# Row-tiled matmuls in the looped MLP chunks of a three-block fp32 transformer kernel

## The chip, the cores and the metric

The kernel runs on one core of one Trainium2 chip. The metric is the device time of one launch in microseconds (us); lower is better. Three runs of the kernel before gave a median of 978.46 us (978.15 to 979.44).

## The reference

Sequence 256, width 1024, everything in fp32. A first block has two layers (attention, then an MLP), a second block has one layer (sparse attention and retention, then a gated FFN). The change touches the MLPs of the two layers of the first block, and nothing else that is computed:

```python
D_MODEL = 1024; SEQ = 256; D_FF = 4 * D_MODEL

def _sq_relu_mlp(h, w_up, w_down):
    u = jax.nn.relu(h @ w_up)          # 256 x 1024 @ 1024 x 4096
    return (u * u) @ w_down            # 256 x 4096 @ 4096 x 1024

x = x + _sq_relu_mlp(_rmsnorm(x, a_norm_mlp[i]), a_w_up[i], a_w_down[i])   # layer 0
x = x + _sq_relu_mlp(_rmsnorm(x, b_norm_mlp[j]), b_w_up[j], b_w_down[j])   # layer 1
```

## The kernel before

Precision. Each fp32 operand is split into a high and a low part, both of type fp32r, which the TensorE multiplies in one pass. A product is three matmuls: high by high, high by low, low by high. Of the weights, ScalarE makes the high part (`split_hi`, L1182; in the loops `split_hi_loop`, L1190, with its instruction at L1194; tile `whi`) and VectorE the low part (`split_lo`, L1689, instruction at L1693; tile `wlo`).

Units. Weights come in units of 512 rows by 512 columns, 1 MB each, over a ring of four slots (`RING = 4`) of three buffers, `raw`, `whi` and `wlo`. SyncE issues the loads. A unit is split three units ahead of its use (`AHEAD = 3`). `prev[u]` is the unit that held the slot before u; the high part of u may be written when the semaphore `mul_done` says that prev[u] has been multiplied (two increments for each unit), and a new load into `raw` waits for both parts of prev[u].

The MLP. D_FF is walked in 8 chunks of 512 (`CHUNKS`). `mlp_units` (L639) orders the units: up(j+1), two units (contraction halves h = 0 and 1), then down(j), two units (output halves c = 0 and 1). up(0) and down(7) are made outside of the loop, by `up_first` and by `mlp_end` (L677). The 7 chunks between are made by `mlp_chunk`, one function for each engine: chunk 0 written out, 1 to 5 in a hardware loop, 6 written out. With two layers that is 14 chunks. "Chunk" below always means one of these 14.

A chunk on TensorE (`mlp_chunk`, L1453). The up part makes the hidden values transposed: for each h, `up_pair` (L1438) fills the two banks of the pair `proj` (Pp), then the two banks of the pair `turn` (Tp). The stationary operand is a 128x128 piece of the weights. For each bank and each k of four, L1445 streams 512 columns (the activations' high and low part side by side) against the high weights; then L1449 streams 256 columns (high activations alone) against the low weights. So a chunk has 32 matmuls of 512 columns and 32 of 256 in its up part. The down part (`half_unit`, L1409, through `products`, L1403, the lines L1405 to L1407) has, for each of two output halves (banks `score` for c = 0, `outp` for c = 1), two token tiles and four k, three matmuls of 512 columns: 48 in all. The stationary operand is there a piece of the activations, and the sums stay in the banks over the chunks. Each of these matmuls contracts 128 rows, uses the whole array, and has a weight load of its own ahead of it.

Around it. When a pair of up banks is complete, ScalarE copies its cross terms (`copy_crosses`, L1216) and VectorE adds, applies relu and squares (`square_relu`, L1708 and L1711); ScalarE and VectorE write the squares' high and low part as the operand of down (`squares_hi`, L1222; `squares_lo`, L1719). TensorE waits for `up_added` before it fills a pair again, for `up_lo` before down(j), and for `lo_done` before each unit.

Of the kernel before, what the change touches and what calls it, by code (L numbers as in the profile page):

```python
# [31 lines left out]
P = 128  # L32
# [6 lines left out]
UK = 4  # L39
# [24 lines left out]

GAINS = ["a_mem_norm", "b_mem_norm", "a_norm_attn", "a_norm_mlp", "kv_norm", "b_norm_attn",
# [34 lines left out]
def build(nc, A, out):  # L100

    UNITS = []

    def unit(w, rows, cols, nk=UK):
# [27 lines left out]
    count.up = 0  # L132
    free = {}

    def add(kind):
        st = Step()
        st.kind = kind
        STEPS.append(st)
        return st

    ctx = ExitStack()
    with ctx:
# [101 lines left out]
        up_copied = sem("up_copied")  # L244
        up_added = sem("up_added")
# [47 lines left out]
        def turn_operand(src, half, gains, ready, set_free, cols=None):  # L293

            st = add("turn_operand")
            st.src, st.half, st.gains, st.ready, st.set_free = src, half, gains, ready, set_free
            st.use, st.hi = [t_use(), t_use()], count.hi
            count.hi += 2
            return st.use
# [31 lines left out]
        def evacuate(u, pieces, scale, slot_free=None, silu=False, bank="P"):  # L331

            st = add("evacuate")
            st.u, st.pieces, st.scale, st.chunk = u, pieces, scale, count.chunk
            st.slot_free, st.silu, st.bank = slot_free, silu, bank
            for t in range(NT):
                free[bank, t] = (chunk_evac, 2 * count.chunk + t + 1)
            count.chunk += 1
            return st

        def rope_chunk(u, slot, table, scale, slot_free, bank="P"):

            st = add("rope_chunk")
            st.u, st.slot, st.table, st.scale, st.slot_free, st.bank = u, slot, table, scale, slot_free, bank
            st.rope, st.read = count.rope, count.rope_read
            for t in range(NT):
                free[bank, t] = (rope_read, 2 * count.rope_read + t + 1)
            count.rope += 1
            count.rope_read += 1
            return st  # L350

        def rope(slot, n, table):
            st = add("rope")
            st.slot, st.n, st.table, st.chunk, st.rope = slot, n, table, count.chunk, count.rope
            count.rope += 1
            return st

        def turn_heads(src, blocks, pieces, ready):

            st = add("turn_heads")  # L360
            st.src, st.blocks, st.pieces, st.ready = src, blocks, pieces, ready
            st.use = [t_use(), t_use()]
            return st.use

        LOW, HIGH, ALL = slice(0, DH), slice(DH, P), slice(0, P)
        tok = lambda t: slice(t * P, (t + 1) * P)
# [65 lines left out]

        def norm(pair):

            st = add("diff_norm")
            st.items, (st.oss, st.ors) = pair, pair[0].both

        def residual(half, bank, u, scale):
            st = add("residual")
            st.half, st.bank, st.u, st.scale, st.r = half, bank, u, scale, count.resid  # L440
            count.resid += 2
            for t in range(NT):
                free[bank, t] = (resid_done, st.r + t + 1)
            return st

        def statistics(src, ready, factor=None, kind="plain"):


            st = add("statistics")
            st.src, st.ready, st.n, st.ss, st.rs = src, ready, count.rstd, col(2), col(2)  # L450
            st.what, st.factor = kind, factor
            if kind == "final":
                st.ss2, st.r2 = col(2), col(2)
            st.sums = count.ss
            count.ss += 2 if kind == "final" else 1
# [195 lines left out]
        def mlp(w_up, w_down, hset, use0, r1, gain):  # L651
# [16 lines left out]
            st.base, st.hset, st.uset, st.up0 = base, hset, 1 - hset, count.up  # L668
# [111 lines left out]
        small = add("small_norm")  # L780
        small.chunk, small.ss, small.rs = ev.chunk, col(2), col(2)
# [45 lines left out]
        def select(ix, first, last):  # L827

            st = add("select")
            st.st, st.rounds = ix, (first, last)  # L830
# [9 lines left out]
        kava = add("shared_kv")  # L840
        kava.use, kava.s, kava.ss, kava.rs = sn_use, s_use((kava_done, 1)), col(2), col(2)
# [36 lines left out]
        qn = add("query_norm")  # L878
        qn.chunk, qn.ss, qn.rs = ev.chunk, col(16), col(16)
        split(qa[1] + AHEAD)  # L880
        last = retention_out(3)
        group = add("group_center")
        group.o, group.mu, group.va, group.rs = last[1], col(16), col(16), col(16)
# [207 lines left out]
        def _(pool):  # L1091
# [19 lines left out]
            sums = [0]  # L1111

            def inverse_of_sums(dst, ss, n, eps=EPS):

                sums[0] += 1
                pool.wait_ge(sum_done, sums[0])
                inverse_rms(dst, ss, n, eps).then_inc(inverse_done, 1)

            for st in STEPS:
# [42 lines left out]
                elif st.kind == "query_norm":  # L1162
                    inverse_of_sums(st.rs, st.ss, DH)
                elif st.kind == "small_norm":
                    inverse_of_sums(st.rs, st.ss, P)
                elif st.kind == "shared_key_sum":
                    inverse_of_sums(st.st.rs, st.st.ss, DH)
                elif st.kind == "group_sum":
                    inverse_of_sums(st.st.rs, st.st.va, DH, GN_EPS)
# [11 lines left out]
        def _(act):  # L1181
            def split_hi(u):  # L1182
# [3 lines left out]
                if prev[u] is not None:  # L1186
                    act.wait_ge(mul_done, 2 * prev[u] + 2)
                act.activation(shaped(whi, u), shaped(raw, u), ACT.Copy).then_inc(hi_done, 1)  # L1188

            def split_hi_loop(u, j, j0, per):  # L1190

                act.wait_ge(landed[slot[u]], j * 32 + (32 * fills[u] - 32 * j0))
                act.wait_ge(mul_done, j * (2 * per) + (2 * prev[u] + 2 - 2 * per * j0))
# [62 lines left out]
            for st in STEPS:  # L1256
# [6 lines left out]
                elif st.kind == "statistics":  # L1263
# [3 lines left out]
                    for t in range(NT):  # L1267
                        ins = act.activation(junk[:, t, :], st.src[:, t, :], ACT.Square, accum_out=st.ss[:, t:t + 1])  # L1268
                    ins.then_inc(ss_done, 1)
# [6 lines left out]
                elif st.kind == "turn_operand":  # L1276
                    for b in range(2):
                        n = st.use[b]
                        act.wait_ge(t_full, n + 1)
                        if st.set_free and b == 0:  # L1280
                            act.wait_ge(mul_done, st.set_free)
                        for g, s, k0 in st.gains:
                            k = k0 + 2 * b
                            if g is None:
                                ins = act.activation(set_hi[s][:, k:k + 2, :], Tb[n % 2][:], ACT.Copy)
                            else:
                                kk = 4 * st.half + 2 * b
                                act.wait_ge(gain_cols, 1 if g < FIRST * KT else 3)
                                for i in range(2):
                                    ins = act.activation(set_hi[s][:, k + i, :], Tb[n % 2][:, i * TOK:(i + 1) * TOK],  # L1290
                                                         ACT.Copy, scale=gcol[:, g + kk + i:g + kk + i + 1])
                        ins.then_inc(t_hi, 1)
                elif st.kind == "evacuate":
                    act.wait_ge(rstd_done, st.scale.n_done)
                    for t in range(NT):
                        act.wait_ge(mul_done, 2 * st.u + t + 1)
                        if st.slot_free and t == 0:
                            act.wait_ge(t_full, st.slot_free)
                        for i, ((a, b), dst) in enumerate(st.pieces):
# [772 lines left out]
```

## Time and profile before

| | |
|---|---|
| median of 3 runs | 978.46 us |
| profiled execution | 978.28 us |
| its span, first to last instruction | 976.6 us |
| mean granted TensorE clock | 0.99 |
| TensorE busy with matmuls | 938.0 us, 96% |
| TensorE busy with weight loads | 790.2 us, 81% |
| VectorE / ScalarE / GpSimd busy | 587.7 / 476.0 / 70.8 us |
| read from memory | 156.12 MB, 161 GB/s |

The profiled execution took 978.28 us, of which 976.6 us are its span. A matmul's record is longer than its share of the engine, because matmuls are pipelined: the record of 512 columns lasts 0.39 us, while the next one starts much earlier. What one matmul costs is therefore read from the distance between starts, or from the chain of waits, where a piece lasts until the next one begins. Weight loads have rows of their own (PEld), beside the matmuls (PE).

### The profile page before, as it was taken

Reading aid. Unit: us, or ns where it says so; the run is one execution under the profiler, and the core shown is the slowest. Engines: PE = TensorE matmul, PEld = TensorE weight load, DVE = VectorE, ACT = ScalarE, POOL = GpSimd, SP = SyncE. Lnnn points to the kernel's source line nnn. Section 1 sums busy time; section 2 is a strip of 40 time slices with the busy share of each in tenths; the row PEclk is TensorE's granted clock in tenths of the full one; section 3 lists DMA queues with packets and bytes.
Section 4 is the critical chain, followed back from the end, with each engine's and each line's share of the span. In section 5 each row is a group of like instructions: output and inputs, shape, how many; then the busy total and the mean of one; then the engine's idle time right before and its main releaser. Section 6 shows DMA issues by size and latency. Waiting matters only on the chain.

```text
span 976.6 us, 13275 instructions
## 1 busy us (share of the span) xinstructions
PE 938.0 (96%) x4758; PEld 790.2 (81%) x4758; DVE 587.7 (60%) x801; ACT 476.0 (49%) x699; POOL 70.8 (7%) x132
## 2 busy tenths in 40 slices
PE   5999989999999999999999999999897999999998
PEld 4788778888888887778888888888776888888887
DVE  3777766756565576543856555558887374545543
ACT  4765565544444365562744444446335364344341
POOL 2101030100000010001100000002133000000000
PEclk9999999999999999899999999999898999999999
DMA  8844223765655443221765565555332055555551
GB/s 278 298 143 132 87 92 131 258 209 174 201 185 191 154 172 130 87 87 45 258 217 193 176 207 178 167 181 191 113 108 85 3 178 199 182 181 198 179 172 43
DMA packets 95435, 157.77 MB, mean 162 GB/s; under 512 B 5928, under 2 KB 37624, under 8 KB 95392
## 3 DMA queue, kind: packets, MB, share of 16 engines
q1 hardware_dynamic: 93872, 155.09, 47.7%
q10 hardware_dynamic: 1488, 2.10, 0.7%
q8 instruction: 27, 0.44, 0.2%
q14 instruction: 16, 0.13, 0.0%
q0 software_dynamic: 32, 0.02, 0.0%
HBM read 156.12 MB, written 1.06 MB: 161 GB/s over the span
## 4 chain that ended last, share of the span: by engine, by line
PE 85%; DVE 6%; ACT 4%; POOL 2%; issue 2%; DMA 1%; SPq 0%; ACTq 0%; DVEq 0%; POOLq 0%
PE proj L1405 8%; PE proj L1407 8%; PE proj L1406 8%; PE turn L1445 5%; PE score L1405 5%; PE proj L1445 5%; PE score L1406 5%; PE score L1407 5%; PE outp L1405 5%; PE outp L1407 5%; PE outp L1406 5%; PE proj L1449 3%; PE turn L1449 3%; PE turn L1432 2%; PE score L1569 2%
## 5 line engine op out<-in xcount | busy, mean ns | idle before, releaser
L1693 DVE TENSOR_TENSOR wlo<-raw,whi 128x2048 fp32r<-128x2048 f32 x145 | 329.7, 2278 | 221.5 <-ACT whi L1194 147.6
L1194 ACT ACTIVATE whi<-raw 128x2048 fp32r<-128x2048 f32 x64 | 122.6, 1916 | 170.0 <-PE outp L1407 57.5
L1405 PE MATMUL proj<-whi,set 128*128 128x512 f32 (+1 forms) x432 | 174.7, 404 | 9.8 <-DVE wlo L1693 7.0
L1188 ACT ACTIVATE whi<-raw 128x2048 fp32r<-128x2048 f32 (+1 forms) x81 | 153.0, 1901 | 47.6 <-PE outp L1407 18.4
L1407 PE MATMUL proj<-whi,set 128*128 128x512 f32 (+1 forms) x432 | 169.5, 392 | 0.0
L1406 PE MATMUL proj<-wlo,set 128*128 128x512 f32 (+1 forms) x432 | 169.2, 392 | 0.0
L1405 PEld LDWEIGHTS proj<-whi,set 128*128 128x128 f32 x432 | 83.0, 192 | 27.1 <-issue 9.2
L1407 PEld LDWEIGHTS proj<-whi,set 128*128 128x128 f32 x432 | 82.6, 191 | 17.6
L1406 PEld LDWEIGHTS proj<-wlo,set 128*128 128x128 f32 x432 | 83.1, 192 | 15.6
L1405 PE MATMUL score<-whi,set 128*128 128x512 f32 x236 | 92.8, 393 | 0.4 <-ACT e L1331 0.4
L1405 PE MATMUL outp<-whi,set 128*128 128x512 f32 x236 | 92.8, 393 | 0.4 <-issue 0.4
L1406 PE MATMUL score<-wlo,set 128*128 128x512 f32 x236 | 92.0, 390 | 0.0
L1407 PE MATMUL score<-whi,set 128*128 128x512 f32 x236 | 92.0, 390 | 0.0
L1407 PE MATMUL outp<-whi,set 128*128 128x512 f32 x236 | 92.0, 390 | 0.0
L1406 PE MATMUL outp<-wlo,set 128*128 128x512 f32 x236 | 91.9, 389 | 0.0
L1290 ACT ACTIVATE set<-turn,gcol 128x256 fp32r<-128x256 f32 x72 | 28.2, 477 | 65.4 <-PE turn L1432 65.4
L1104 POOL TENSOR_SCALAR newton<-stat 128x2 f32<-128x2 f32 (+1 forms) x18 | 14.7, 816 | 622.0 <-ACT wT L1268 488.9
L1331 ACT ACTIVATE e<-score,stat 128x256 f32<-128x256 f32 (+1 forms) x80 | 33.7, 427 | 50.9 <-DVE stat L1869 50.9
L1445 PE MATMUL turn<-set,whi 128*128 128x512 f32 x224 | 56.1, 392 | 0.0
L1445 PE MATMUL proj<-set,whi 128*128 128x512 f32 x224 | 55.8, 391 | 0.0
L1405 PEld LDWEIGHTS outp<-whi,set 128*128 128x128 f32 x236 | 44.3, 188 | 9.7 <-DVE set L1846 0.8
L1407 PEld LDWEIGHTS score<-whi,set 128*128 128x128 f32 x236 | 44.3, 188 | 9.5
(207 smaller groups left out, 1240.0 us busy)
## 6 DMA issues: line engine op xcount, KB each, us to landing
raw<-in_a_w_up SPq DMA_DIRECT2D x32, 512.0 KB, 4.3
raw<-in_a_w_down SPq DMA_DIRECT2D x32, 512.0 KB, 4.5
raw<-in_b_w_up SPq DMA_DIRECT2D x32, 512.0 KB, 4.2
raw<-in_b_w_down SPq DMA_DIRECT2D x32, 512.0 KB, 4.4
raw<-in_w_gate SPq DMA_DIRECT2D x22, 512.0 KB, 4.0
raw<-in_w_up SPq DMA_DIRECT2D x22, 512.0 KB, 4.9
raw<-in_w_down SPq DMA_DIRECT2D x22, 512.0 KB, 3.9
raw<-in_a_w_in SPq DMA_DIRECT2D x20, 512.0 KB, 6.6
```

What stands on the lines that cost most here:

```text
L1188: act.activation(shaped(whi, u), shaped(raw, u), ACT.Copy).then_inc(hi_done, 1)
L1194: act.activation(shaped(whi, u), shaped(raw, u), ACT.Copy).then_inc(hi_done, 1)
L1290: ins = act.activation(set_hi[s][:, k + i, :], Tb[n % 2][:, i * TOK:(i + 1) * TOK], ACT.Copy, scale=gcol[:, g + kk + i:g + kk + i + 1])
L1331: ins = act.activation(dst, src, ACT.Exp, bias=it.nm[:, c:c + 1], scale=SCALE, accum_out=it.rs[:, c:c + 1])
L1405: pe.matmul(out_, hi, wh, start=start, stop=False)
L1406: pe.matmul(out_, hi, wl, start=False, stop=False)
L1407: return pe.matmul(out_, lo, wh, start=False, stop=stop)
L1432: ins = pe.transpose(Tb[n % 2][:, at:at + P], src(t, k), ident[:])
L1445: pe.matmul(pair[:, i, :], wh[:, k, cols], moving, start=h == 0 and k == 0, stop=False)
L1449: ins = pe.matmul(pair[:, i, 0:TOK], wl[:, k, cols], set_hi[hset][:, UK * h + k, :], start=False, stop=h == 1 and k == UK - 1)
L1569: ins = pe.matmul(S[:, o:o + it.n], headq[:, it.q, c, tok(it.t)], it.k[:, 0:it.n], start=True, stop=it.kind == "mem")
L1693: dve.tensor_tensor(shaped(wlo, u), shaped(raw, u), shaped(whi, u), ALU.subtract).then_inc(lo_done, 1)
```

## The change

In the 14 chunks each matmul with 128 contracted rows becomes two with 64, one on partitions 0 to 63 and one on 64 to 127, that is, in the upper and the lower half of the array. The two halves stand next to each other in the program, each with a weight load of its own, and they work on different banks at any time. `in_row_tiles` walks four slots in four steps: in step n the upper half works on slot n and the lower half on slot n + 2 (modulo 4), so that each slot gets both halves' sums, two steps apart. In up the slots are the four banks of `proj` and `turn` for one h; in down they are the four banks of both output halves, so both down units are used from the first step to the last. Number of columns, operands' types and the number of chunks stay as they are. Up_first, mlp_end and everything outside of the chunks keep their matmuls.

The waits follow: a new semaphore `tile_steps` counts the first two steps of each up half, `mul_done` the last two; a step that comes back to a slot waits until the step before last is complete. Both up pairs must be free (`up_added` of both) before the first step, both down units must be split before down starts, and `consumed` (ScalarE) frees both down units only when the whole down part is done.

Besides, steps that covered both token tiles or both banks are now listed as one step for each (`turn_operand`, `evacuate`, `rope_chunk`, `turn_heads`, `residual`, `select`, `statistics` with a new `square_sum`), and `program(engine)` may reorder steps by a table `MOVES`, which is empty. Each engine's instructions stay in the order that they had.

```diff
+            def in_row_tiles(slots, run, start, ready, finished):
+                for n in range(4):
+                    ready(n)
+                    for both in zip(run(slots[n], HALF[0], start and n < 2, n >= 2),
+                                    run(slots[(n + 2) % 4], HALF[1], start and n < 2, n >= 2)):
+                        for operands, opens, closes in both:
+                            ins = pe.matmul(*operands, start=opens, stop=closes)
+                    finished(n, ins)
+
+            def up_tiles(u, h, hset, step, multiplied):
+                wh, wl = shaped(whi, u), shaped(wlo, u)
+                def run(slot, rows, start, last):
+                    q, i = slot
+                    cols, bank = slice((2 * q + i) * P, (2 * q + i + 1) * P), (Pp, Tp)[q][:, i, :]
+                    for k in range(UK):
+                        both = sets[hset][rows, UK * h + k, :, :].rearrange("p s n -> p (s n)")
+                        yield (bank, wh[rows, k, cols], both), start and k == 0, False
+                    for k in range(UK):
+                        yield (bank[:, 0:TOK], wl[rows, k, cols], set_hi[hset][rows, UK * h + k, :]), False, \
+                            last and h == 1 and k == UK - 1
+                def ready(n):
+                    if n >= 2:
+                        pe.wait_ge(tile_steps, step + (n - 1))
+                    elif h == 1:
+                        pe.wait_ge(mul_done, multiplied + (n + 1))
+                def finished(n, ins):
+                    ins.then_inc(tile_steps if n < 2 else mul_done, 1)
+                in_row_tiles([(0, 0), (1, 0), (0, 1), (1, 1)], run, h == 0, ready, finished)
+
+            def down_tiles(u, lhs, start, multiplied):
+                def run(slot, rows, start, last):
+                    c, t = slot
+                    wh, wl = shaped(whi, u + c), shaped(wlo, u + c)
+                    for k in range(UK):
+                        for m, (side, w) in enumerate(((set_hi, wh), (set_hi, wl), (set_lo, wh))):
+                            yield ((banks["SO"[c]][t][:], side[lhs][rows, UK + k, tok(t)], w[rows, k, :]),
+                                   start and k == 0 and m == 0, False)
+                def ready(n):
+                    if n >= 2:
+                        pe.wait_ge(mul_done, multiplied + (n - 1))
+                def finished(n, ins):
+                    ins.then_inc(mul_done, 1)
+                in_row_tiles([(0, 0), (0, 1), (1, 0), (1, 1)], run, start, ready, finished)
...
             def mlp_chunk(st, j, peel, first):
...
                 for h in range(2):
                     u = u0 + h
                     pe.wait_ge(lo_done, at(u + 1, 4))
-                    for q, pair in enumerate((Pp, Tp)):
-                        if h == 0 and first and q == 0:
-                            for t in range(NT):
-                                wait(st.freed[t])
-                        elif h == 0 and not first:
-                            pe.wait_ge(up_added, j * 2 + (st.up0 + q + 1))
-                        up_pair(u, h, q, st.hset, pair)
+                    if h == 0 and first:
+                        for t in range(NT):
+                            wait(st.freed[t])
+                    elif h == 0:
+                        pe.wait_ge(up_added, j * 2 + (st.up0 + 2))
+                    up_tiles(u, h, st.hset, step + 2 * h, multiplied)
                 pe.wait_ge(up_lo, j * 2 + (st.up0 + 2))
-                for c, b in enumerate("SO"):
-                    u = u0 + 2 + c
-                    pe.wait_ge(lo_done, at(u + 1, 4))
-                    if first:
-                        pe.wait_ge(up_added, st.up0 + 2 - c)
-                    for t in range(NT):
-                        half_unit(u, t, st.uset, UK, banks[b][t], first, False)
+                pe.wait_ge(lo_done, at(u0 + 4, 4))
+                if first:
+                    pe.wait_ge(up_added, st.up0 + 2)
+                down_tiles(u0 + 2, st.uset, first, multiplied + 4)
...
+            def consumed(u):
+                return 2 * u + (4 if u in BOTH else 2)      # BOTH: the first down unit of each chunk
...
-                    act.wait_ge(mul_done, 2 * prev[u] + 2)
+                    act.wait_ge(mul_done, consumed(prev[u]))
```

## Rows read from the trace of the kernel before

**Rows 1.** The page: busy time by engine (share, instructions), chain of waits by engine.
```profile
PE 938.0 (96%) x4758; PEld 790.2 (81%) x4758; DVE 587.7 (60%) x801; ACT 476.0 (49%) x699; POOL 70.8 (7%) x132
...
PE 85%; DVE 6%; ACT 4%; POOL 2%; issue 2%; DMA 1%; SPq 0%; ACTq 0%; DVEq 0%; POOLq 0%
```

**Rows 2.** Windows: 7 chunks of each layer, then one chunk; length, busy by engine, clock.
```profile
171.90:326.30 154.40, 154.40 (x786) 131.96 (x785) 95.18 (x77) 71.12 (x61) 3.27 (x6) 1.00 0.60 201
477.60:632.00 154.40, 154.40 (x786) 131.93 (x785) 95.18 (x77) 70.94 (x61) 3.12 (x5) 1.00 0.59 195
216.05:238.10 22.05, 22.05 (x113) 18.85 (x112) 12.79 (x10) 9.80 (x8) 0.00 (x0) 1.00 0.57 190
```

**Rows 3.** Chain of waits, up part of one chunk: start, length, what.
```profile
216.24 1.81 PE proj L1445 x8
218.06 0.95 PE proj L1449 x8
219.01 1.84 PE turn L1445 x8
220.85 0.95 PE turn L1449 x8
```

**Rows 4.** Timeline, matmuls and weight loads in a down part.
```profile
300.21 0.39 PE L1405 MATMUL outp<-whi,set 128*128 128x512 f32 x1
300.22 0.19 PEld L1406 LDWEIGHTS outp<-wlo,set 128*128 128x128 f32 x1
300.44 0.39 PE L1406 MATMUL outp<-wlo,set 128*128 128x512 f32 x1
300.44 0.19 PEld L1407 LDWEIGHTS outp<-whi,set 128*128 128x128 f32 x1
300.67 0.39 PE L1407 MATMUL outp<-whi,set 128*128 128x512 f32 x1
...
300.89 0.39 PE L1405 MATMUL outp<-whi,set 128*128 128x512 f32 x1
```

**Rows 5.** Timeline and chain, plain fp32 scores (256 columns, two cycles each).
```profile
79.07 1.89 PE L1569 MATMUL score<-memkv,qk 128*128 128x256 f32 x8
...
79.24 1.73 PE score L1569 x8
```

**Rows 6.** Timeline and chain, short matmuls with a full weight load each.
```profile
95.05 1.89 PE L1614 MATMUL outp<-memkv,wT 128*128 128x64 f32 x16
...
95.21 1.73 PE outp L1614 x16
96.94 0.88 PE turn L1590 x8
```

**Rows 7.** Timeline, TensorE's first instructions after it had waited.
```profile
381.13 0.19 PEld L1405 LDWEIGHTS proj<-whi,set 128*128 128x128 f32 x1 [1.58 <-issue]
381.16 0.47 PE L1405 MATMUL proj<-whi,set 128*128 128x512 f32 x1 [1.37 <-DVE zq L1771]
381.24 0.19 PEld L1406 LDWEIGHTS proj<-wlo,set 128*128 128x128 f32 x1
```

**Rows 8.** Timeline, ScalarE and VectorE in a chunk that begins at 304.06.
```profile
304.55 1.92 ACT L1188 ACTIVATE whi<-raw 128x2048 fp32r<-128x2048 f32 x1 [3.58 <-PE outp L1407]
...
306.50 2.29 DVE L1693 TENSOR_TENSOR wlo<-raw,whi 128x2048 fp32r<-128x2048 f32 x1 [3.21 <-ACT whi L1188]
...
308.71 1.29 DVE L1719 TENSOR_TENSOR set<-zq,set 128x512 fp32r<-128x512 f32 x2
...
310.11 1.92 ACT L1188 ACTIVATE whi<-raw 128x2048 fp32r<-128x2048 f32 x1 [2.60 <-PE turn L1449]
...
316.95 1.28 DVE L1711 SCALAR_TENSOR_TENSOR zq<-zq 128x512 f32<-128x512 f32 x2
...
323.12 2.29 DVE L1693 TENSOR_TENSOR wlo<-raw,whi 128x2048 fp32r<-128x2048 f32 x1 [1.48 <-ACT whi L1188]
```

**Rows 9.** The page, part 6: DMA issues, KB each, us to landing.
```profile
raw<-in_a_w_down SPq DMA_DIRECT2D x32, 512.0 KB, 4.5
```

More of the change, by code:

```diff
@@ L63 @@
 SMALL = 292
+MOVES = {}
 GAINS = ["a_mem_norm", "b_mem_norm", "a_norm_attn", "a_norm_mlp", "kv_norm", "b_norm_attn",
@@ L102, in build @@
     UNITS = []
+    BOTH = set()
     def unit(w, rows, cols, nk=UK):
@@ L131, in build, with program @@
     count.decayed, count.w, count.dots, count.rope_read = 0, 0, 0, 0
-    count.up = 0
+    count.up, count.inverse, count.sums, count.tile_steps = 0, 0, 0, 0
     free = {}
+    kinds = {}
     def add(kind):
         st = Step()
-        st.kind = kind
+        kinds[kind] = kinds.get(kind, -1) + 1
+        st.kind, st.name = kind, f"{kind} {kinds[kind]}"
         STEPS.append(st)
         return st
+    def program(engine):
+        steps = list(STEPS)
+        at = {st.name: st for st in STEPS}
+        for name, ahead_of in MOVES.get(engine, ()):
+            steps.remove(at[name])
+            steps.insert(steps.index(at[ahead_of]), at[name])
+        return steps
     ctx = ExitStack()
@@ L453, in statistics @@
                 st.ss2, st.r2 = col(2), col(2)
-            st.sums = count.ss
-            count.ss += 2 if kind == "final" else 1
+            st.sums = count.ss + 1
+            count.ss += 3 if kind == "final" else 2
             count.rstd += 2 if kind == "final" else 1
@@ L827, in select @@
         def select(ix, first, last):
-            st = add("select")
-            st.st, st.rounds = ix, (first, last)
+            for r in range(first, last):
+                st = add("select")
+                st.st, st.round = ix, r
         def step(kind, of):
@@ new lines, in _ @@
+                    b = st.b
+                    n = st.use[b]
+                    act.wait_ge(t_full, n + 1)
+                    if st.set_free and b == 0:
+                        act.wait_ge(mul_done, st.set_free)
+                    for g, s, k0 in st.gains:
+                        k = k0 + 2 * b
+                        if g is None:
+                            ins = act.activation(set_hi[s][:, k:k + 2, :], Tb[n % 2][:], ACT.Copy)
+                        else:
+                            kk = 4 * st.half + 2 * b
+                            act.wait_ge(gain_cols, 1 if g < FIRST * KT else 3)
+                            for i in range(2):
+                                ins = act.activation(set_hi[s][:, k + i, :], Tb[n % 2][:, i * TOK:(i + 1) * TOK],
+                                                     ACT.Copy, scale=gcol[:, g + kk + i:g + kk + i + 1])
@@ L1791, in rope_in_place @@
[L1791 to L1798 removed]
+                t = st.t
@@ new lines, in rope_from_bank @@
+                dve.wait_ge(rope_read, 2 * st.read + t + 1)
+                dve.tensor_tensor(z, z, rt[:, t, :], ALU.add).then_inc(rope_done, 1)
+            def rope_in_place(st):
+                t = st.t
+                n = 2 * st.rope + t
+                dve.wait_ge(rope_done, n - 1)
+                dve.wait_ge(chunk_evac, 2 * (st.chunk - 1) + t + 1)
+                z, t1, t2 = zq[:, st.slot, t, 0:st.n], rt[:, t, 0:st.n], rt[:, t, st.n:2 * st.n]
+                behind(turn_pairs(st, t, st.n // DH, z, 1.0, t1, t2))
+                dve.tensor_tensor(z, t1, t2, ALU.add).then_inc(rope_done, 1)
```

283 lines of the change are left out of this document (136 added, 147 removed).

## The prediction

> **What bounds the kernel now.** I read the page first, then windows over the changed stretch, then the chain of waits inside it, then the timeline. The page says that TensorE is busy for 96% of the span and carries 85% of the chain [rows 1]. The windows say more: in the two stretches that the change touches, 154.40 us each, and in a single chunk of 22.05 us, TensorE is busy for the whole time, at a granted clock of 1.00 (the 2.4 GHz level), while VectorE has work for 12.79 us of 22.05 and ScalarE for 9.80 [rows 2]. So 308.8 us of the span are set by how fast matmuls follow one another, and by nothing else. The chain gives that pace: in up, 8 matmuls of 512 columns take 1.81 to 1.84 us (226 to 230 ns each) and 8 of 256 take 0.95 us (119 ns each) [rows 3]; in down the starts are 0.227 us apart [rows 4]. The sum closes: 32 x 229 + 32 x 119 + 48 x 226.7 ns = 22.0 us, the chunk of [rows 2].
>
> What of a pace is columns? At 2.4 GHz, 512 columns take 213.3 ns and 256 take 106.7. So each matmul pays 12 to 16 ns on top, which I call the hand-over. It is not the loading of weights: the next load begins with the matmul and its record is over after 0.19 us, before the next matmul starts at 0.227 [rows 4]. Nor does every matmul pay it: plain fp32 scores of 256 columns at two cycles a column, again 213.3 ns, each with a new load, follow at 1.73/8 = 216 ns, a hand-over of 3 ns [rows 5]. Both rows have a fresh 128x128 stationary operand; they differ in the rate at which columns are fed, one or half a column a cycle. I take it that the full-rate stream has a gap at its start that the slower stream hides. Over the 14 chunks the hand-overs come to 14 x (22.05 - 80 x 0.2133 - 32 x 0.1067) = 22 us. That is all that the change can give back, since the columns stay: two halves with 64 rows each do in 512 columns what one matmul did.
>
> **The change part by part.** (1) Pairs. If the halves run at once, a pair still needs 213.3 or 106.7 ns of columns. While one half hands over, the other can be in mid-stream, and feeding and control see a steady flow. No row shows two matmuls in different halves, so the price of a pair is bounded: from 213.3 ns (hand-over gone) to 227 (each half pays its own), if the halves overlap; the nearest row to a hidden gap is the 216 ns of [rows 5], and I take that for 512 columns. Gain: 227 - 216 = 11 ns x 80 x 14 = 12.3 us. (The 2 to 3 ns that up's matmuls pay above 227 I leave.)
>
> (2) Pairs of 256 columns. They have 107 ns for two loads and two matmuls. Two prices could bind. Each half has a load of its own, and full loads follow at 1.73/16 = 108 ns, or 0.88/8 = 110 [rows 6]: fine if the halves load at the same time. And four instructions must be issued: after a wait, the first load and its matmul start 0.03 us apart [rows 7], so four take some 112 to 124 ns. I take 116 ns, 3 less than the 119 of [rows 3]: 3 x 32 x 14 = 1.3 us. Ends: 109 (gain 4.5) and 124 (loss 2.2).
>
> (3) Entering and leaving. Each layer goes from whole-array matmuls to halves and back: 4 changes. If the array must be empty each time, one costs at most what a record lasts beyond its pace, 0.39 - 0.23 = 0.16 us [rows 4]; 4 x 0.16 = 0.65 us, which I charge in full. The low end is 0. The Trainium skill (TensorEngine Tiling (Array Packing), Key Properties) says that a change of tiling mode drains the engine; no row before shows such a change.
>
> (4) New waits. A step waits for the step before last, which was issued at least one step (8 pairs of up, about 1.3 us) earlier, and whose matmuls are complete 0.16 us after their columns. Such a wait is met before it is asked, so it costs nothing, as long as the queue behind it holds work. Behind each stands TensorE's whole remaining stream; ScalarE waits for what it counts. The pair `proj` is complete one step (1.3 us) later than now, `turn` as now. `up_added` of both is wanted at the first step; the squares that follow it end at 318.2, in the down part of the same chunk, 8 us before the next up [rows 8]. Cost nothing.
>
> (5) Later release of the first down unit. Its slot is now free at the end of the chunk and not 5.4 us before. Today its low part is made at 323.12, near the end of the chunk, and the second down unit's at 306.50 to 308.79, early in the next [rows 8]. After: both high parts then both low parts come at the beginning of the chunk, 0.5 + 1.9 + 2 x 2.29 = 7.0 us in, and the squares' low part 1.3 us later, at 8.3. Down starts 11.2 us in (10.6 when faster). Slack 2.3 us or more; the next high part on ScalarE (310.11, 6 us in) is wanted a whole chunk later. Loads into `raw` start some 5 us later and land in 4.5 us [rows 9] with over 10 us to go. Nothing, but if the cover were gone, each us would count 14 times. The relisted steps change no order: nothing.
>
> Sum against the profiled execution: 978.28 - 12.3 - 1.3 + 0.65 = **965.3 us**. The profiled execution lies 0.18 us below the median of the runs; I leave that out.
>
> **What the skill says of pairs.** TensorE: Matmul & The Clock Gate (Measured speedup vs the span model) has tiles in different row groups start about 4 ns apart, four row tiles giving 3.07 times one; by that halves do overlap, and a pair is one matmul plus 4 ns once, not per pair. No run here shows it yet. The same page (LDWEIGHTS) prices a load by its columns alone, 128/1.2 = 107 ns for 64 rows as for 128; the 108 ns of [rows 6] agrees for 128 rows. By that figure two loads one after the other are 213 ns, and an estimate with 213 for every pair is 978.28 + 14 x (32 x 94 - 32 x 16 - 48 x 13) ns, 1005 us. Its picture of row tiles shows the loads overlapping instead. So one page feeds both the forecast and the third rival.
>
> **The rivals.** *Each half pays its own hand-over.* If the gap belongs to the stream in a half, the pair costs 227 and 119 as before, and only (3) is left: 978.28 + 0.65 = 978.9 us. For it: each half is itself a sequence of load and matmul at full rate, as today. Against: [rows 5] shows that the gap is not in swapping the weights.
>
> *Loads one after the other* (slower). If there is a single path for loads and a load of 64 rows takes as long as one of 128, a pair costs at least 2 x 110 = 220 ns [rows 6]. For 512 columns that is hidden (-7 in down, -9 in up), for 256 columns it is the bound: +101. 14 x (32 x 101 - 32 x 9 - 48 x 7) ns = +36.5 us, with (3) 1015.4 us; with 108 or 112 ns for a load, 1009 to 1022. It decides from the point where a pair's two loads take longer than its columns. For it: no two loads in the trace are closer than 108 ns. Against: none of them went to different halves.
>
> *The halves don't run at once.* Each half puts out all 128 columns' sums, so a pair writes twice what one matmul wrote. If only one stream can leave the array at a time, each pair is two matmuls: +308.8 us, 1287 us; if they overlap in part, anything between. This is also the case in which the change doesn't do what it says. Nothing in the trace excludes it.
>
> **How the numbers follow.** The forecast (halves overlap, hand-over at least partly hidden) gets 0.47, own range 957 (all 22 us) to 973; own hand-over 0.17; loads in turn 0.18; no or partial overlap 0.18. With the last left out the range reaches from 956 to 1022. What a measurement of this kernel can tell from no change is about 0.2%, 2 us. Faster takes the forecast's 0.47 and a little of the second case: 0.48; same 0.15; slower 0.37.
>
> **What would show it.** In the changed profile a chunk should last 22.05 - 80 x 0.011 - 32 x 0.003 = 21.1 us. Upper and lower matmul should start a few ns apart, pairs of 512 columns 216 ns apart (own hand-over: 227; loads in turn: 220), pairs of 256 at 116 (loads in turn: 220, the clearest sign). Without overlap a matmul of the lower half starts 213 ns after its partner. VectorE's and ScalarE's busy time should stay; a wait of TensorE for `wlo` or `set` in the chunks would show (5) wrong, a hole of more than 0.2 us at the edges of the two stretches (3). The prediction is wrong above all if the hand-over is the stream's own, or if two loads don't overlap.

## The result and the profile after

The changed kernel takes 979.72 us (median of 20 runs, 978.33 to 982.39) against 977.98 us (20 runs, 976.49 to 979.54) for the kernel before. The ratio is 1.002, with a 95% interval of 1.0013 to 1.0027: slower by 1.3 to 2.6 us, a difference of 0.2%, and certainly not faster. The profiled execution took 979.03 us, with a span of 977.3.

The page of the changed kernel, its busy times (share, instructions):

```profile
PE 938.7 (96%) x6326; PEld 788.5 (81%) x6326; DVE 586.5 (60%) x801; ACT 474.3 (49%) x699; POOL 70.7 (7%) x132
```

There are 1568 more matmuls and as many more weight loads than in [rows 1] (112 for each of 14 chunks), and yet neither busy time has moved by more than 2 us: the added work lies beside the other half's. The windows over the seven chunks of the first layer and over one chunk of the changed kernel (length, then busy time of TensorE's matmuls, its weight loads, VectorE, ScalarE and GpSimd, then granted clock, DMA share and rate):

```profile
171.17:326.30 155.13, 155.13 (x1570) 131.50 (x1570) 92.47 (x76) 68.32 (x60) 3.12 (x5) 1.00 0.57 200
...
193.50:215.63 22.13, 22.13 (x227) 18.79 (x226) 12.69 (x10) 9.68 (x8) 0.00 (x0) 1.00 0.56 191
```

Against [rows 2]: 155.13 us in place of 154.40, and 22.13 in place of 22.05 for a chunk. TensorE is busy all the time, the clock is 1.00, and VectorE and ScalarE have the work that they had. No wait has come in.

The timeline of the changed kernel at the beginning of a down part, matmuls of the two halves (the upper one writes `score`, the lower one `outp`):

```profile
204.54 0.39 PE L1500 MATMUL score<-whi,set 64*128 64x512 f32 x1
204.54 0.39 PE L1500 MATMUL outp<-whi,set 64*128 64x512 f32 x1
204.78 0.39 PE L1500 MATMUL score<-wlo,set 64*128 64x512 f32 x1
204.78 0.39 PE L1500 MATMUL outp<-wlo,set 64*128 64x512 f32 x1
205.01 0.39 PE L1500 MATMUL score<-whi,set 64*128 64x512 f32 x1
205.01 0.39 PE L1500 MATMUL outp<-whi,set 64*128 64x512 f32 x1
```

and its weight loads there:

```profile
204.54 0.18 PEld L1500 LDWEIGHTS score<-wlo,set 64*128 64x128 f32 x1
204.55 0.18 PEld L1500 LDWEIGHTS outp<-wlo,set 64*128 64x128 f32 x1
```

The halves start within 0.01 us of each other, and so do their loads. So the change does exactly what it says, and two loads in different halves don't queue for one another. But from pair to pair it is 0.24 and 0.23 us. The hand-over is still there, in both halves at the same moment, and in this place it is even a little longer than the 0.227 us of [rows 4]. The chain over the first up half (h = 0) of a chunk of the changed kernel (start, length, what; each x16 is one step, that is eight pairs):

```profile
193.50 1.38 PE proj L1500 x16
194.88 1.40 PE turn L1500 x16
196.28 1.41 PE proj L1500 x16
197.69 1.40 PE turn L1500 x16
```

Four steps take 5.59 us; the first four pieces of [rows 3], the same work, take 5.55.

### The profile page after: what moved, and what is told of

The parts are those of the page before. It is cut to its first block, busy times and chain, and to the rows that moved or that the text cites. A ratio compares the mean times of both kernels' runs of the same rounds, so it can differ in the third digit from the quotient of the medians.

```text
span 977.3 us, 16473 instructions
## 1 busy us (share of the span) xinstructions
PE 938.7 (96%) x6326; PEld 788.5 (81%) x6326; DVE 586.5 (60%) x801; ACT 474.3 (49%) x699; POOL 70.7 (7%) x132
## 4 chain that ended last, share of the span: by engine, by line
PE 85%; DVE 6%; ACT 4%; POOL 2%; issue 2%; DMA 0%; SPq 0%; ACTq 0%; DVEq 0%; POOLq 0%
PE proj L1444 8%; PE proj L1446 8%; PE proj L1445 8%; PE proj L1500 8%; PE turn L1500 8%; PE score L1500 8%; PE outp L1500 8%; PE score L1444 3%; PE score L1446 3%; PE score L1445 3%; PE outp L1444 3%; PE outp L1446 3%; PE outp L1445 3%; PE turn L1471 2%; PE score L1659 2%
## 5 line engine op out<-in xcount | busy, mean ns | idle before, releaser
L1445 PE MATMUL proj<-wlo,set 128*128 128x512 f32 (+1 forms) x432 | 168.8, 391 | 0.0
L1500 PE MATMUL score<-whi,set 64*128 64x512 f32 x448 | 139.8, 387 | 0.0
L1500 PE MATMUL outp<-whi,set 64*128 64x512 f32 x448 | 139.8, 387 | 0.0
L1445 PEld LDWEIGHTS proj<-wlo,set 128*128 128x128 f32 x432 | 82.6, 191 | 15.5
L1500 PEld LDWEIGHTS outp<-whi,set 64*128 64x128 f32 x448 | 82.5, 184 | 8.8
L1500 PEld LDWEIGHTS score<-whi,set 64*128 64x128 f32 x448 | 82.5, 184 | 8.6
L1500 PE MATMUL score<-wlo,set 64*128 64x512 f32 x224 | 86.7, 387 | 0.0
L1500 PE MATMUL outp<-wlo,set 64*128 64x512 f32 x224 | 86.7, 387 | 0.0
L1500 PE MATMUL turn<-set,whi 64*128 64x512 f32 x448 | 61.2, 391 | 0.0
L1500 PE MATMUL proj<-set,whi 64*128 64x512 f32 x448 | 61.0, 390 | 0.0
L1444 PE MATMUL outp<-whi,set 128*128 128x512 f32 x124 | 49.2, 397 | 0.6 <-issue 0.6
L1444 PE MATMUL score<-whi,set 128*128 128x512 f32 x124 | 49.3, 397 | 0.4 <-ACT e L1370 0.4
```

The lines of the kernel that those rows point to most:

```text
L1444: pe.matmul(out_, hi, wh, start=start, stop=False)
L1445: pe.matmul(out_, hi, wl, start=False, stop=False)
L1500: ins = pe.matmul(*operands, start=opens, stop=closes)
```

## The experiments

Three questions were open: whether the gap belongs to each half or to something shared, what the gap is, and where the 0.08 us of a chunk come from.

**The halves half a matmul apart.** Edit of the changed kernel, in the down part:

```diff
-                    for both in zip(run(...upper...), run(...lower...)): ...
+                    upper, lower = list(run(...)), list(run(...))
+                    ...                                          # from the second chunk of a layer on
+                    (out_, weights, moving), opens, closes = lower[0]
+                    parts = [((out_[:, c:c + 256], weights, moving[:, c:c + 256]), opens and c == 0, closes)
+                             for c in (0, 256)]
+                    order = [upper[0], parts[0]]
+                    for i in range(1, len(upper)):
+                        order += [lower[i], upper[i]]
+                    order.append(parts[1])
```

> The changed kernel, but in the down part the lower half runs half a matmul behind the upper one: its first matmul of each step is made as two of 256 columns, one at the start and one at the end of the step. In the changed kernel both halves begin within 4 ns of each other, so they also hand over at the same moment. Theory 1 (each half's stream has its own gap of 13 ns): upper matmuls still start 227 ns apart, each down step costs about 11 ns more for the extra matmul, a chunk goes from 22.13 to about 22.17 us. Theory 2 (the gap sits in a part that serves both halves and is only exposed because they hand over together): starts of one half go to about 216 ns, a chunk to about 21.6 us, the time falls by some 7 us. Only the changed chunks 1 to 6 of each layer have the offset.

It took 982.74 us in one run, 3.0 us above the changed kernel's median. Its chunks account for little of that: five of them, from 194.38 to 305.16, take 22.16 us each, near the 22.17 of Theory 1. The rest lies outside the chunks; this is a single run, and no cause is shown for it. The timeline in a down part of this run:

```profile
236.82 0.39 PE L1510 MATMUL outp<-wlo,set 64*128 64x512 f32 x1
236.88 0.39 PE L1510 MATMUL score<-wlo,set 64*128 64x512 f32 x1
237.04 0.39 PE L1510 MATMUL outp<-whi,set 64*128 64x512 f32 x1
237.11 0.39 PE L1510 MATMUL score<-whi,set 64*128 64x512 f32 x1
237.27 0.39 PE L1510 MATMUL outp<-whi,set 64*128 64x512 f32 x1
237.34 0.39 PE L1510 MATMUL score<-whi,set 64*128 64x512 f32 x1
```

The offset didn't hold at the intended 119 ns. It drifted from step to step, from 3 ns to somewhat over 100; here it is 60 to 70 ns one way and 160 the other. That is enough: while one half hands over, the other is in mid-stream, and still `outp` starts at 236.82, 237.04, 237.27 and `score` at 236.88, 237.11, 237.34, 0.22 to 0.23 us apart. Over a longer stretch the figure is sharper: `outp` starts 11 times from 236.14 to 238.40, which is 0.227 us each and not 0.216. Theory 2, on which the forecast stood, falls.

**The upper half alone.** Edit of the changed kernel:

```diff
-                    for both in zip(run(slots[n], HALF[0], ...), run(slots[(n + 2) % 4], HALF[1], ...)):
-                        for operands, opens, closes in both:
-                            ins = pe.matmul(*operands, start=opens, stop=closes)
+                    for operands, opens, closes in run(slots[n], HALF[0], start, True):
+                        ins = pe.matmul(*operands, start=opens, stop=closes)
```

> The changed kernel without the lower half: half of every contraction of the chunks is left out, and the upper half makes the same matmuls at the same places. Theory 1 (the gap is the stream's own): starts stay 227 and 119 ns apart and a chunk at 22.0 to 22.1 us, and the slow starts after each run of 256 columns (233 to 236 ns) should shrink if they come from the number of instructions, since there are half as many. Theory 2 (two halves share feed or loads): the upper half alone goes below 227, down to 216.

The chain of this run (x8 are the eight matmuls of a step), then its windows over a chunk:

```profile
194.03 1.38 PE proj L1498 x8
195.41 1.40 PE turn L1498 x8
196.81 1.41 PE proj L1498 x8
...
194.03:216.16 22.13, 22.13 (x114) 18.55 (x113) 12.69 (x10) 9.68 (x8) 0.00 (x0) 1.00 0.56 190
```

These are to the hundredth the times of both halves together, with half the instructions (the whole launch took 980.93 us, in one run). So the second half costs nothing, and taking it away gives nothing. My second expectation here, that the slow starts come from the number of instructions, was wrong. They are all still there: a step takes 1.40 and 1.41 us behind the first one's 1.38.

**The gap and the weight load.** Edit of the kernel before, in the down part of chunks 1 to 5:

```diff
-                        half_unit(u, t, st.uset, UK, banks[b][t], first, False)
+                        ...
+                        few = slice(t * P, t * P + 64)
+                        for k in range(UK):
+                            ins = products(banks[b][t][0:64, :], set_hi[st.uset][:, UK + k, few],
+                                           set_lo[st.uset][:, UK + k, few], wh[:, k, :], wl[:, k, :], False, False)
```

> The kernel before, but in chunks 1 to 5 of each layer the down matmuls load only 64 of the 128 stationary columns; half of down's output is left out, and 512 columns are streamed as before. Theory 1 (the gap belongs to the moving stream): starts stay 227 ns apart. Theory 3 (the gap comes from the weight load or the swap to the new weights, and grows with the columns loaded): starts go to about 220 ns, a chunk's down part from 10.9 to 10.6 us.

The timeline of this run:

```profile
229.97 0.40 PE L1407 MATMUL score<-whi,set 128*64 128x512 f32 x1
230.20 0.39 PE L1405 MATMUL score<-whi,set 128*64 128x512 f32 x1
...
231.34 0.40 PE L1407 MATMUL score<-whi,set 128*64 128x512 f32 x1
```

Six starts from 229.97 to 231.34 make 228 ns each. Single distances go from 224 to 236 ns, with a mean of 230: a little more than 227, with a load that is shorter (0.13 us in place of 0.19). The launch took 979.51 us, in one run. So the gap is not a price of loading columns; why the starts became uneven is open.

**The gap and the bank.** Edit of the kernel before: consecutive matmuls of 512 columns go to the two banks of a pair in turn (in up the same):

```diff
-                    for t in range(NT):
-                        half_unit(u, t, st.uset, UK, banks[b][t], first, False)
+                    for k in range(UK):
+                        for m, (side, w) in enumerate(((set_hi, wh), (set_hi, wl), (set_lo, wh))):
+                            for t in range(NT):
+                                ins = pe.matmul(banks[b][t][:], side[st.uset][:, UK + k, tok(t)], w[:, k, :], ...)
```

> The kernel before, whole array, but every next 512-column matmul of the chunks goes to the other bank of the pair: the same products in another order. So far neither the other half (changed kernel), nor its absence, nor a shorter load moved the gap of 13 ns. Theory 4 (the gap comes from adding to the bank that the matmul before still writes): starts fall to 214 to 216 ns, a chunk by about 0.9 us. Theory 1 (it is in feeding a stream at one column a cycle): 227 ns and a chunk of 22.05 us as before.

The ratio to before is 0.9999 (0.9989 to 1.0008), a chunk is 22.05 us. Theory 4 falls.

**The gap and the bytes of a column.** Three runs, each an edit of the kernel before in the down parts of chunks 1 to 5 of a layer:

```diff
# bf16, step of four bytes:
+                        top = lambda ap, n: ap.bitcast(BF16).rearrange("p (n two) -> p n two", two=2)[:, :, 1]
+                        ... products(..., top(set_hi[...], P), top(set_lo[...], P), top(wh[:, k, :], COLS), top(wl[:, k, :], COLS))
# bf16, dense:
+                        dense = identb[:].unsqueeze(1).broadcast_to([P, 4, P])
+                        ... products(..., top(set_hi[...], P), top(set_lo[...], P), dense, dense)
# fp32r, the same 128 columns four times:
+                        again = lambda ap: ap[:, 0:P].unsqueeze(1).broadcast_to([P, 4, P])
+                        ... products(..., set_hi[...], set_lo[...], again(wh[:, k, :]), again(wl[:, k, :]))
```

> The kernel before, but in chunks 1 to 5 of each layer the down matmuls read the upper two bytes of the same operands as bf16; the lower bytes are left out. Same numbers of matmuls, columns and loads. If the gap of 13 ns belongs to fp32r at full rate, starts go to about 216 ns as for the plain fp32 rows; if every full-rate stream with a fresh load has it, they stay at 227. A read with a stride could also make them slower, which the trace would show as columns taking longer than 213 ns.

> As the run with bf16 operands (starts 225 ns apart, operands with a step of four bytes), but the moving operand of the down matmuls in chunks 1 to 5 is a dense bf16 tile of 128 columns, read four times over: the weights' part of these products is left out, number of matmuls, columns and loads stay. If the gap comes from the bytes that a column needs from memory, dense bf16 reads half as many and starts fall to about 216 ns, as for the plain fp32 rows with half the rate. If any stream at one column a cycle has the gap, they stay at 225.

> The kernel before, but in chunks 1 to 5 of each layer the down matmuls read the first 128 columns of their fp32r operand four times over, in place of 512 different ones; the other three quarters of the weights are left out. The dense bf16 run, 216 ns a start, changed two things against the stepped bf16 run: two bytes for a column in place of four, and 128 columns read again and again. If the bytes for a column set the gap, fp32r read in this way stays at 227 ns. If reading the same place again closes it, starts fall to 216 here too.

Timeline of the run with stepped bf16:

```profile
229.97 0.39 PE L1406 MATMUL score<-wlo,set 128*128 128x512 bf16 x1
...
231.32 0.39 PE L1406 MATMUL score<-wlo,set 128*128 128x512 bf16 x1
```

of the run with dense bf16:

```profile
229.64 0.38 PE L1407 MATMUL score<-identb,set 128*128 128x512 bf16 x1
...
230.93 0.38 PE L1407 MATMUL score<-identb,set 128*128 128x512 bf16 x1
```

and of fp32r read four times over:

```profile
229.80 0.39 PE L1405 MATMUL score<-whi,set 128*128 128x512 f32 x1
...
231.16 0.39 PE L1405 MATMUL score<-whi,set 128*128 128x512 f32 x1
```

Six starts each: 1.35, 1.29 and 1.36 us, that is 225, 215 and 227 ns; over a whole down part the dense run has 216. The launches took 979.04, 972.60 and 976.45 us, one run each. With four bytes between columns, fp32r or bf16, the gap is there; with two bytes it is 2 to 3 ns. The weight loads don't explain that: they last 0.10 us in both bf16 runs. For fp32r, reading the same place again doesn't close it. Nor is the rate of columns alone the cause, since dense bf16 has one column a cycle too. [rows 5], four bytes at half a column a cycle and 216 ns, fits the same reading: at the 2.4 GHz level a matmul pays 9 to 11 ns more when its stream moves on by four bytes in each partition in every cycle. The price is one for each matmul and not for each column, since 256 columns pay no less (119 to 120 ns against 106.7). Halving the rows, as the change does, leaves the bytes per partition and cycle as they were. What is not separated: the dense tile is an identity matrix in another place of the memory, so its data and its place differ as well as its density. And what in the chip makes the gap is not shown.

**The order in up, whole array.** Two edits of the kernel before. First the order of the changed kernel, four matmuls of 512 columns and then four of 256 for each bank; second 16 and 16 for each unit. The first edit:

```diff
                 for i in range(2):
                     for k in range(UK):
                         pe.matmul(pair[:, i, :], wh[:, k, cols], moving, ...)
-                for i in range(2):
-                    ...
                     for k in range(UK):
                         ins = pe.matmul(pair[:, i, 0:TOK], wl[:, k, cols], ...)
```

> The kernel before with whole-array matmuls, but in up each bank gets its four of 512 columns and then its four of 256, as the changed kernel has it, in place of eight and eight for a pair of banks. The trace of the changed kernel has its 512-column pairs 228 to 236 ns apart after each run of 256, and there are eight such runs in a chunk in place of four. Theory A (the 0.08 us that a chunk became longer come from this alternation): a chunk goes from 22.05 to about 22.13 us with whole-array matmuls, and the time rises by about 1 us. Theory B (they come from the halves, 3 to 4 ns for each pair's offset or the doubled number of instructions): a chunk stays at 22.05.

> The kernel before, but each up unit makes all 16 of its matmuls of 512 columns, then all 16 of 256: two runs of 256 in a chunk in place of four. Theory A (starts are slow after each run of 256): a chunk falls from 22.05 to about 22.00 us and the time by 0.7 us, less than can be told with certainty. Theory B: a chunk stays at 22.05.

Up's beginning in two chunks of the first run, from its chain (L1445 are the 512 columns, L1447 the 256):

```profile
193.59 0.91 PE proj L1445 x4
194.50 0.47 PE proj L1447 x4
194.97 0.93 PE proj L1445 x4
...
215.72 0.91 PE proj L1445 x4
```

and in two chunks of the second:

```profile
193.94 1.81 PE proj L1471 x8
...
215.96 1.81 PE proj L1471 x8
```

A chunk is 22.13 us with four and four, 22.02 with 16 and 16, and 22.05 as it was. The first ratio follows, 1.0014 (1.0005 to 1.0024); the second, 0.9996 (0.9987 to 1.0005), can't be told from no change. So chunks of whole-array matmuls in the changed kernel's order are as long as its own. Theory A holds: behind a run of 256 four matmuls of 512 take 0.93 us and not 0.91, the single starts being up to 0.24 us apart, and the changed kernel has eight such runs in a chunk where there were four.

**That order in halves.** Edit of the changed kernel: `up_tiles` makes its pairs of 512 on the four slots in turn, then its pairs of 256 on them (`for part in range(2): for n in range(4): ...`, with waits on `tile_steps` for each step).

> The changed kernel, but each up unit makes all its pairs of 512 columns on the four slots in turn and then all its pairs of 256: two runs of 256 in a chunk in place of eight. If the 0.07 us by which a chunk of the changed kernel is longer come from the slow starts after each run of 256, a chunk falls from 22.13 to 22.01 us, as in the whole-array kernel with this order, and the time to within 0.1% of before, with the four changes between whole and split array (0.21 us each by the run with down alone) left on top. If the halves cost something of their own, a chunk stays above 22.05.

Two chunks begin at 215.65 and 237.67 in the chain of this run:

```profile
215.65 0.91 PE proj L1538 x8
...
237.67 0.91 PE proj L1538 x8
```

22.02 us, as with the whole array in this order, and a ratio of 1.000 (0.9991 to 1.001). In the same order a chunk of halves and one of the whole array last the same.

**Down alone in halves.** Edit of the changed kernel: `up_pair` of before in place of `up_tiles`.

```diff
-                    up_tiles(u, h, st.hset, step + 2 * h, multiplied)
+                    for q, pair in enumerate((Pp, Tp)):
+                        ...
+                        up_pair(u, h, q, st.hset, pair)
```

> The changed kernel with up made by whole-array matmuls as before, and only down in halves. Each chunk enters and leaves the split array once, 28 changes in place of 4. If a change costs 0.16 us, as the prediction charged, a chunk rises by 0.33 us to about 22.4 and the time by 4.5 us; if it costs nothing, a chunk is 22.05 to 22.1 us. In the trace the distance from the last matmul of one kind to the first of the other shows it directly: 119 or 227 ns without a cost, 275 to 390 ns if the array is emptied.

The timeline at both changes of a chunk:

```profile
205.61 0.50 PE L1500 MATMUL score<-whi,set 64*128 64x512 f32 x1
205.94 0.39 PE L1500 MATMUL score<-wlo,set 64*128 64x512 f32 x1
...
216.40 0.39 PE L1500 MATMUL score<-whi,set 64*128 64x512 f32 x1
216.71 1.20 PE L1484 MATMUL proj<-set,whi 128*128 128x512 f32 x4
```

and the beginning of two chunks in its chain:

```profile
194.30 2.05 PE proj L1484 x8
...
216.78 2.05 PE proj L1484 x8
```

The median is 985.43 us (4 runs) and the ratio 1.0075 (1.0058 to 1.0092), the largest loss of all. The last pair and the first whole matmul are 0.31 us apart and not 0.227, and the second matmul after a change comes after 0.33. From chunk to chunk it is 216.78 - 194.30 = 22.48 us in the chain, 0.43 more than before for two changes: 0.21 us each. Over 14 chunks that is 6.0 us, within the interval of the ratio (5.7 to 9.0 us). I had charged 0.16. The Trainium skill (TensorEngine Tiling (Array Packing), Key Properties) says that a change of tiling mode drains the engine; it gives no price. These rows agree in that a change costs time, 0.21 us; whether the engine is empty in between they don't show.

**Quarters.** Edit of the changed kernel: `quarters = [run(slots[q], slice(32 * q, 32 * q + 32), ...) for q in range(4)]`, made in turn by fours.

> The changed kernel with four quarters of 32 rows, each at its own bank, in place of two halves that change banks: every bank gets only a quarter of its contraction, the rest is left out. A group of four has eight instructions. If four run at once and only columns and the gap count: 227 and 119 ns, a chunk of 22.1 us. If issuing an instruction costs 28 to 31 ns, as the prediction took it from the first starts after a wait, groups of 256 columns need 224 to 248 ns, those of 512 up to 248, and a chunk becomes 25 to 27 us. If loads of different quarters are made one after the other at 108 ns, every group takes over 430 ns and a chunk 48 us.

My arithmetic for the chunk was wrong: with a quarter of the contraction there are 28 groups in a chunk and not 112, so TensorE waits once in each chunk, up to 4.7 us, for VectorE's `set`, and VectorE, busy for 12.5 of a chunk's 13.4 us, sets the pace (the launch took 866.55 us, in one run). The distances say what was asked. Timeline of an up part at full clock, four quarters a group:

```profile
200.90 0.41 PE L1500 MATMUL proj<-set,whi 32*128 32x512 f32 x2
200.92 0.39 PE L1500 MATMUL turn<-set,whi 32*128 32x512 f32 x2
...
201.37 0.27 PE L1500 MATMUL proj<-set,wlo 32*128 32x256 f32 x1
...
201.48 0.27 PE L1500 MATMUL proj<-set,wlo 32*128 32x256 f32 x1
...
201.60 0.28 PE L1500 MATMUL proj<-set,wlo 32*128 32x256 f32 x1
```

Groups of 256 columns, eight instructions each (four loads, four matmuls), start 0.11 to 0.12 us apart: issuing costs 15 ns an instruction at most. The 28 to 31 ns that the prediction took as the price of issue, from [rows 7], are not one. The same run shows the gap from another side. In a down part that begins after TensorE had waited 4.57 us for VectorE's `set`, the granted clock is 0.50, the 1.2 GHz level; timeline, then the window around it:

```profile
209.30 0.64 PE L1500 MATMUL score<-whi,set 32*128 32x512 f32 x2
209.32 0.63 PE L1500 MATMUL outp<-whi,set 32*128 32x512 f32 x2
209.73 0.64 PE L1500 MATMUL score<-wlo,set 32*128 32x512 f32 x2
...
208.90:210.90 2.00, 2.00 (x24) 1.67 (x20) 2.00 (x4) 0.00 (x0) 0.00 (x0) 0.50 0.95 344
```

Here groups of 512 columns are 0.43 us apart. Over eight of them, from 207.60 to 211.01, it is 0.427 us each, and 512/1.2 is 0.427: there is no gap at half the clock, though the stream still moves on by four bytes in every, now longer, cycle.

## Why the prediction was wrong

It said 965.3 us, a gain of 13, with a range of 956 to 1022. The result, 979.72, lies inside the range, which was wide enough to hold it by way of its rivals, but the forecast of a gain is wrong. The rival *each half pays its own hand-over*, 978.9 us at 0.17, is what happened, with 1.0 us on top that no case had.

- *What bounds the kernel*: right. TensorE sets the two stretches before and after, and the hand-over of 12 to 16 ns is real. The observation that plain fp32 doesn't pay it [rows 5] was the right one to make. The reading of it, that any stream at one column a cycle has the gap, was wrong: dense bf16 at one column a cycle pays 2 to 3 ns. What divides the four kinds of stream is the number of bytes by which they move on in a cycle: four with the gap (fp32r, stepped bf16), two without it (plain fp32, dense bf16).
- *Part (1), pairs of 512 columns*: the step that failed. From a gap that a slower stream doesn't have I went to a gap that is hidden if another half is in mid-stream. Nothing in the rows said so, and the 216 ns of [rows 5] were a row of another rate and not of another neighbour. The term of 12.3 us was 0: pairs of 512 columns start 227 ns apart, the runs with the offset (0.227 us) and with one half alone (a chunk of 22.13 us either way) show that the gap is each half's own. It fits that a half moves on by four bytes per partition and cycle like the whole.
- The same step had a second hole: the two halves stand side by side in the program and start within 0.01 us, so one was never in mid-stream when the other handed over. That could be read from the diff.
- *Part (2), pairs of 256 columns*: loads in different halves don't queue and issue is no bound, so neither of the two prices applied. The pairs start 0.12 us apart, as the matmuls in [rows 3] do. 1.3 us became nothing. The rival *loads one after the other*, and with it the estimate of 1005 us, is excluded: both loads start within 0.01 us, and pairs of 256 columns start 0.12 us apart and not 0.22. *The halves don't run at once* is excluded by the same rows.
- *What was left out*: in (1) I set aside the 2 to 3 ns that up's matmuls pay above 227. They are a cost of the order: each run of 256 columns is followed by slow starts, and the change doubled these runs. This term was put at nothing without a reason. 14 x 0.074 us (22.127 to 22.053 us from chunk to chunk) are 1.0 us.
- *Part (3)*: right in kind, 0.21 us in place of 0.16 each; 4 x 0.21 = 0.85 us.
- *Parts (4) and (5)*: right. TensorE has no new wait in the chunks. In the chunk of the changed kernel that begins at 215.47, the squares' low part is done at 223.31 and down begins at 226.67: a cover of 3.4 us where 2.3 was forecast.

The sum of what the runs showed, 1.0 + 0.85 = 1.9 us, would be a ratio of 1.0019; measured is 1.002 (1.0013 to 1.0027), and 1.74 us between the medians. The run in halves with 16 and 16 agrees: 14 x -0.04 + 0.85 = +0.3 us, which is too little to be told in its interval of 0.9991 to 1.001.

No version beat the kernel before by more than the runs can tell: the whole array with 16 and 16 has shorter chunks by 0.04 us, 0.6 us in all, and a ratio of 0.9996 with an interval around 1.

## What to carry to other kernels

When each matmul already fills the array, splitting it gave nothing here: each part still streams all the columns and pays the same gap. So look for the cause of the gap (here, as far as the runs separate it, the bytes that a column needs in a cycle) and not for something to hide it behind. A row that is cheaper for one reason (rate) is no bound for a change of another kind (neighbour). Keep changes between whole and split array out of loops (0.21 us each here). Don't alternate short and long matmuls more than is needed: doubling the runs cost 0.14% here, halving them gave less than these runs can tell.

## What was not expected of the hardware

- A stream of one column a cycle with four bytes from column to column pays 12 to 13 ns between matmuls at the 2.4 GHz level (227 ns for 512 columns, fp32r; 225 for stepped bf16), one with two pays 2 to 3 (216 ns, dense bf16, an identity matrix). At the 1.2 GHz level fp32r had no gap (0.427 us, in quarters).
- Two halves of the array run beside each other with their own weight loads, at no cost: 22.13 us a chunk with one half or both. So do four quarters: groups of 256 columns start 0.11 to 0.12 us apart.
- Each change between whole array and halves costs 0.21 us (22.48 us a chunk with two changes, 22.05 with none).
- After a run of 256-column matmuls the next ones of 512 start up to 0.24 us apart, with one half, two halves or the whole array. With shorter loads (64 columns) the starts stay uneven, 230 ns on average. Why is open.
